# Two-layer hybrid diffusion step: a new order in layer 0's start, a weight tile split in two, value products over fewer query columns, and sums at other steps

## The chip, the cores and the metric

The kernel runs on one core of one Trainium2 chip. The metric is the device time of one execution in microseconds, lower is better; the engines are TensorE (PE), VectorE (DVE), ScalarE (ACT), GpSimd (POOL) and the queue that issues most transfers, SyncE (SP).

## What is computed

Two layers over 1152 tokens (1024 latent tokens on a 16 x 64 grid, 128 context tokens) of width 1024. Cut to what matters here:

```python
def modulate(x, cond, g, w_mod, b_mod):
    mod = jax.nn.silu(cond) @ w_mod + b_mod
    shift, scale, gate = jnp.split(mod[:, None, :], 3, axis=-1)
    return rmsnorm(x, g) * (1 + scale) + shift, gate

def latent_layer(x, c, ...):
    parts, gate = project(x, c, g, w_mod, b_mod, w_in)      # modulate(x) @ w_in, 3584 columns
    ya, yb = branches_ab(parts[:7], w_s, b_s, w_conv)        # gated MLP over positions; gated convolution
    yc = window_attn(cq, ck, cv, kc, vc, sink) * silu(cz)    # mixer C: +-128 tokens
    yd = neighbourhood_attn(dq, dk, dv, kd, vd, rpb) * silu(dz)   # mixer D
    return x + gate * (jnp.concatenate([ya, yb, yc, yd], -1) @ w_out)
```

In mixer D a query in grid row r sees eight rows of keys, from clip(r - 4, 0, 8) on, and 16 columns, beside the context keys:

```python
    def one_row(r):
        rs = jnp.clip(r - kr // 2, 0, rows - kr)             # kr = 8, rows = 16
        k_nb = jnp.take(kg, rs + jnp.arange(kr), axis=1)[:, :, col_idx]
```

After both layers comes one RMSNorm.

## The kernel before

**Products.** Everything is float32. The large projections run as three products of a rounded and a rest part: `w_hi` x `h_hi`, `w_hi` x `h_lo`, `w_lo` x `h_hi`, in the fp32r format. A weight tile is 128 output columns by 8 blocks (k) of 128 inputs; tokens go in three chunks (c) of 384. Tile w is loaded by SP into a raw buffer, ACT casts it to `w_hi[:, w % 2]` in two halves of four k (`high_half`, L281), POOL subtracts for `w_lo` (`low_half`, L287). Two tiles can be in work. A step is one tile and one chunk: 24 matmuls of 384 columns on L1088. Steps 0 to 5 are tiles 0 and 1, later three steps to a tile; the 24 steps of the output projection follow, numbered st = 0 to 23.

**The start of layer 0** (`sync_start`, `pool_start`, `scalar_start`, `tensor_start`, `vector_start`). x is squared on ACT and added on DVE, PE sums it over partitions (`sums`, L606), DVE takes 1/sqrt (`rsqrt`, L193 to L202) and writes nine diagonals (L707, signal `pro_norm[0]`), PE spreads each over all partitions with a matmul by ones (`spread`, L583, into banks 3, 4 and 5, signal `pro_norm[1]`), and ACT copies the three banks to SBUF (L547, `pro_copied`). For each k DVE then makes scaled x (L663), ACT `h_hi` (L530), DVE `h_lo` (L672) and PE the products of tiles 0 and 1 (`project`, L596), of which the one with n = 1 writes banks 3 to 5. Between them PE makes the modulation rows of block k + 3 (`make_rows`, L564), ACT copies them (`copy_row`, L524), PE turns them (`turn_row`, L575), and DVE takes them in (`take_mods`, L649 to L654). `AHEAD` is 3, so the rows of blocks 0, 1 and 2 are made ahead of the loop over k. w_mod blocks are loaded into three buffers, block k after block k - 3 has been used. POOL has only `low_half` of tiles 0 and 1 here.

**Attention.** Scores of two pairs of heads and query blocks are made at the end of steps `S_AT`, DVE adds bias and takes the maximum (L1542), ACT takes exp, DVE normalises (L1552), two steps later (`V_AT`) PE turns the probabilities ahead of k = 0 to 3 (`turn_probs`, L1108), ACT copies them, and at the end of the step PE multiplies by values (`values`, L1117), each of two heads into its half of the 128 PSUM partitions; then DVE gates (`gate_pair`, L1564). In mixer D a unit is 8 grid rows x 16 columns of queries against 12 rows x 32 columns of keys, taken in three blocks of four rows behind one block of context; masked probabilities are zero.

**Other modulation.** DVE multiplies 24 blocks of w_mod with the condition at steps `MOD_AT` (`multiply`, L1383 and L1380), the blocks loaded by SP one by one as the two buffers come free; PE sums each third over partitions at `SUM_AT` (`mod_sums`, L1143) in the middle of the step, ahead of k = 4, DVE copies it (L1395), PE turns it at `TURN_MOD_AT`, DVE adds it in (L1404). These small products share PSUM bank 7 with the value products, so each waits for the reader of the one before. Layer 1 uses only the middle third of the tables.

**Norm at the end of a layer.** From st = 1 on DVE adds squares of the new x (L1623). In step 16 PE sums the first six token blocks (`sum_tokens`, L187), DVE makes 1/sqrt and diagonals (`make_rstd`, L1365), and PE spreads them in step 17 (L1235). Every order is written out by hand; an engine does its instructions in that order and waits on semaphores.

Of the kernel before, what the change touches and what calls it, by code (L numbers as in the profile page):

```python
# [31 lines left out]
P = 128  # L32
# [5 lines left out]
KT = D_MODEL // P  # L38
# [77 lines left out]
def build(nc, xT, cond, w_mod, w_mod0, b_mod, norm_g, final_g, w_tiles, w_sT, b_s, w_conv, sink, rpb,  # L116
          cckT, ccv, cdkT, cdv, ident_c, rope_c, band_c, row_c, col_c, yT, sckT, scvT, sdkT, sdvT):
    with ExitStack() as ctx:
# [96 lines left out]
        masks_in = sem("masks_in")  # L215
        mod_taken = sem("mod_taken")
        wmod_in = [sem(f"wmod_in{i}") for i in range(3)]
        cond_tanh = sem("cond_tanh")
# [56 lines left out]

        def high_half(act, layer, w):
            s = signals[layer]
            loaded = (s.w_loaded0, s.w_loaded1, s.w_loaded2, s.w_loaded3)[raw_at(w)]
            act.wait_ge(loaded, 16 * loads_until(layer, w))
            for a, b in w_halves(w):  # L280
                nc.scalar.copy(w_hi[:, w % 2, a:b], RAW[raw_at(w)][:, a:b]).then_inc(s.hi_ready, 1)  # L281
# [7 lines left out]


        PARTS = ((LAT, 0), (CTX, 1))

# [58 lines left out]
        BLOCKS = [len(unit_values(u)) for u in range(NU)]  # L351


        BANK_S, BANK_O = 3, 7
# [7 lines left out]
        mod_row = (xy[:, 2, D_MODEL:T], xy[:, 3, D_MODEL:T])  # L362
        MOD_AT = [8, 10, 11, 13, 14, 16, 17, 18] + [23, 24, 25, 26, 28, 29, 30, 31] + [37, 38, 39, 40, 41, 42, 44, 45]
        SUM_AT = {20: (0, 0), 22: (0, 1), 33: (1, 0), 35: (1, 1), 52: (2, 0), 54: (2, 1)}
        TURN_MOD_AT = {21: (0, 0), 23: (0, 1), 34: (1, 0), 36: (1, 1), 53: (2, 0), 55: (2, 1)}

# [146 lines left out]
        def pool_start(pool):  # L513
            low_half(pool, 0, 0)
            low_half(pool, 0, 1)
            pool.wait_ge(masks_in, 16 * 3)

        def scalar_start(act):
# [6 lines left out]

            def make_high(k):
                for i, part in enumerate(first_parts(k)):
                    act.wait_ge(signals[0].scaled, first_count(k, i))
                    for cols, cnd in part:
                        last = nc.scalar.activation(h_hi[:, k, cols], first_scaled[k % 2][:, cols], ACT.Identity,  # L530
                                                    bias=mods[:, 0, k, cnd:cnd + 1])
                    last.then_inc(signals[0].h_hi_ready, 1)

# [10 lines left out]
            copy_row(1)  # L544
            for c in range(NCH):
                act.wait_ge(pro_norm[1], 3 * (c + 1))
                nc.scalar.copy(first_rstd[:, cols_of(c)], psum[:, RSTD_BANK + c, 0:CH]).then_inc(pro_copied, 1)  # L547
            copy_row(2)
            for k in range(KT):
                make_high(k)  # L550
                if k + AHEAD < KT:
                    copy_row(k + AHEAD)

        def tensor_start(pe):
# [31 lines left out]
            def project(k, c):  # L586

                if c == 0 and k % 4 == 0:
                    pe.wait_ge(s.lo_ready, k // 4 + 1)
                if k == 0 or c != 1:  # L590
                    pe.wait_ge(s.h_lo_ready, first_count(k, c if k == 0 else c // 2))
                for n in range(2):
                    if k % 4 == 0 and c == 0 and n == 1:
                        pe.wait_ge(s.lo_ready, 2 + k // 4 + 1)
                    for w, h in ((w_hi, h_hi), (w_hi, h_lo), (w_lo, h_hi)):
                        last = nc.tensor.matmul(psum[:, 3 * n + c, 0:CH], w[:, n, k, :], h[:, k, cols_of(c)],  # L596
                                                start=(k == 0 and w is w_hi and h is h_hi),
                                                stop=(k == KT - 1 and w is w_lo), skip_group_check=True)
                    if k == KT - 1:
                        last.then_inc(s.chunk_done, 1)  # L600

            def sums(c):
# [14 lines left out]
            make_rows(1)  # L617
            turn_row(1)
            for c in range(NCH):
                spread(c)  # L620
            make_rows(2)
            pe.wait_ge(pro_copied, NCH)
            for k in range(KT):
# [250 lines left out]
        def scalar_layer(act, layer):  # L874
# [162 lines left out]
            for g, (n, c) in enumerate(STEPS):  # L1037
# [5 lines left out]
                for w in range(2, N_W):  # L1043
                    if HIGH_AT[w] == g:
                        act.wait_ge(s.chunk_done, g + 1)
                        high_half(act, layer, w)
                for u in units_of(S_AT.get(g, ())):
# [34 lines left out]
        def tensor_layer(pe, layer):  # L1082
# [29 lines left out]
            def values(p):  # L1112

                u = 2 * p
                for b in range(BLOCKS[u]):
                    for r in range(2):
                        last = nc.tensor.matmul(psum[64 * r:64 * r + 64, BANK_O, values_at(p)], unit_values(u + r)[b],  # L1117
                                                prob[:, (u + r) % PROBS, b * P:(b + 1) * P], start=(b == 0),
                                                stop=(b == BLOCKS[u] - 1), skip_group_check=True)
# [182 lines left out]
            for st, (f, c) in enumerate(OUT_STEPS):  # L1302
# [5 lines left out]
                for at, k in enumerate(order):  # L1308
                    if at == 4:
                        if st == 16:  # L1310
                            sum_tokens(s, 0, 6, squares_in(15))
                    if at == 7 and st == 17:
# [519 lines left out]
```

## Time and profile before

| | |
|---|---|
| median of 3 runs | 1209.03 us (1208.07 to 1211.74) |
| profiled execution, time | 1208.2 us |
| its span, first to last instruction | 1206.4 us |
| mean granted TensorE clock | 0.994 of full speed |
| PE busy | 1162.4 us, 96% |
| DVE busy | 614.7 us, 51% |
| ACT busy | 443.1 us, 37% |
| POOL busy | 365.9 us, 30% |
| chain that ended last | 84% on PE, 67% on L1088 |

A busy share is an average; the rows below say where an engine waits and for whom. PE's matmuls are pipelined, so one matmul of 384 columns shows some 0.34 us although the next starts 0.17 us after it. A float32 matmul appears as two records.

### The profile page before, as it was taken

The numbers are of one execution on the slowest core, as the hardware profiler recorded it, in microseconds if no ns is written. First come the engines' busy times: TensorE is split into PE (matmuls) and PEld (weight loads), VectorE is DVE, ScalarE is ACT, GpSimd is POOL, SyncE is SP. The second block draws the span as 40 slices with busy tenths as digits, with TensorE's granted clock in tenths as the row PEclk, the third lists the DMA queues.
The fourth block names the chain that finished last, engine by engine and source line by source line (L and its number), as shares of the span: only waits on it lengthen the run. The fifth ranks groups of instructions, "written<-read, shape, count | busy, mean of one in ns | idle before, by whom it ended". The sixth has DMA issues, their size and how long they took to land.

```text
span 1206.4 us, 20224 instructions
## 1 busy us (share of the span) xinstructions
PE 1162.4 (96%) x8098; PEld 1100.1 (91%) x8098; DVE 614.7 (51%) x1419; ACT 443.1 (37%) x1004; POOL 365.9 (30%) x284
## 2 busy tenths in 40 slices
PE   2989999999999999999999999999999999999996
PEld 2689989989999999999999999998999999999996
DVE  5747856764764532152385354675344451334256
ACT  4433445544453111152254344544445311124231
POOL 1023231155351221223352223124434212223342
PEclk9999999999999999999999999999999999999998
DMA  8522221332320112235461111222121111222334
GB/s 347 208 64 101 96 74 56 112 109 90 115 70 18 36 52 88 80 95 163 135 201 50 63 45 38 87 87 69 62 69 37 36 36 36 87 92 80 123 109 157
DMA packets 42861, 110.80 MB, mean 92 GB/s; under 512 B 6032, under 2 KB 21520, under 8 KB 41488
## 3 DMA queue, kind: packets, MB, share of 16 engines
q1 hardware_dynamic: 38736, 105.58, 25.7%
q10 hardware_dynamic: 4032, 3.93, 0.9%
q8 instruction: 64, 1.05, 0.4%
q14 instruction: 29, 0.24, 0.1%
HBM read 99.27 MB, written 10.22 MB: 91 GB/s over the span
## 4 chain that ended last, share of the span: by engine, by line
PE 84%; DVE 3%; issue 0%; ACT 0%; DVEq 0%; ACTq 0%
PE psum L1088 67%; PE psum L1117 5%; PE psum L1100 5%; PE psum L1108 4%; PE psum L1125 1%; PE psum L1134 1%; DVE xy L1383 1%; PE psum L1235 0%; DVE slots L1472 0%; PE psum L1143 0%; DVE slots L1670 0%; DVE slots L1469 0%; DVE prob L1552 0%; DVE slots L1476 0%; PE psum L187 0%
## 5 line engine op out<-in xcount | busy, mean ns | idle before, releaser
L1088 PE MATMUL psum<-h_hi,w_hi 128*128 128x384 f32 x1680 | 586.3, 349 | 2.7 <-POOL w_lo L287 2.7
L1088 PE MATMUL psum<-h_hi,w_lo 128*128 128x384 f32 x1680 | 563.9, 336 | 0.0
L1088 PE MATMUL psum<-h_lo,w_hi 128*128 128x384 f32 x1680 | 562.8, 335 | 0.0
L287 POOL TENSOR_TENSOR w_lo<-w_raw,w_hi 128x512 fp32r<-128x512 f32 x144 | 203.2, 1432 | 647.4 <-ACT w_hi L281 647.3
L1088 PEld LDWEIGHTS psum<-h_hi,w_hi 128*128 128x128 f32 x1680 | 316.1, 188 | 21.1 <-issue 17.3
L1088 PEld LDWEIGHTS psum<-h_lo,w_hi 128*128 128x128 f32 x1680 | 316.7, 189 | 0.0
L1088 PEld LDWEIGHTS psum<-h_hi,w_lo 128*128 128x128 f32 x1680 | 315.9, 188 | 0.0
L281 ACT CAST w_hi<-w_raw 128x512 fp32r<-128x512 f32 x144 | 81.8, 618 | 166.1 <-PE psum L1088 146.6
L983 ACT ACTIVATE prob<-prob,stat 128x512 f32<-128x512 f32 (+2 forms) x144 | 96.4, 671 | 90.9 <-DVE stat L1542 90.7
L990 ACT COPY prob<-psum 128x512 f32<-128x512 f32 (+1 forms) x144 | 75.3, 544 | 27.4 <-PE psum L1108 26.9
L1383 DVE SCALAR_TENSOR_TENSOR xy<-xy,silu 128x1024 f32<-128x1024 f32 x56 | 83.1, 1524 | 3.0 <-DMA xy<-in_w_mod 1.7
L1552 DVE TENSOR_SCALAR prob<-prob,stat 128x512 f32<-128x512 f32 (+1 forms) x144 | 81.2, 564 | 6.5
L1636 DVE SCALAR_TENSOR_TENSOR xy<-psum,mods,slots 128x384 f32<-128x384 f32 (+1 forms) x64 | 31.6, 513 | 103.6 <-PE psum L1088 103.5
L1108 PE MATMUL psum<-ident,prob 128*128 128x128 f32 x512 | 79.3, 272 | 0.7 <-DVE prob L1552 0.7
L1564 DVE SCALAR_TENSOR_TENSOR xy<-psum,xy 128x128 f32<-128x128 f32 x72 | 17.8, 286 | 113.4 <-PE psum L1117 112.7
L1442 DVE SCALAR_TENSOR_TENSOR xy<-slots,psum 128x384 f32<-128x384 f32 x48 | 26.6, 554 | 94.6 <-ACT slots L973 93.5
L848 POOL TENSOR_TENSOR table<-row_mask,table 128x384 f32<-128x384 f32 x48 | 47.1, 982 | 82.8 <-DMA table<-in_rpb 82.8
L946 ACT ACTIVATE slots<-psum 128x384 f32<-128x384 f32 x60 | 29.1, 492 | 110.7 <-PE psum L1088 109.4
L1108 PEld LDWEIGHTS psum<-ident,prob 128*128 128x128 f32 x512 | 64.2, 141 | 5.8 <-issue 1.3
L973 ACT ACTIVATE slots<-psum 128x384 f32<-128x384 f32 x48 | 23.6, 492 | 120.2 <-PE psum L1088 120.2
L287 POOL TENSOR_TENSOR w_lo<-table,w_hi 128x512 fp32r<-128x512 f32 x32 | 44.0, 1395 | 64.0 <-ACT w_hi L281 64.0
L1117 PE MATMUL psum<-prob,slots 128*64 128x128 f32 x896 | 63.0, 276 | 0.0
(119 smaller groups left out, 1077.8 us busy)
## 6 DMA issues: line engine op xcount, KB each, us to landing
w_raw<-in_w_tiles SPq DMA_DIRECT2D x72, 512.0 KB, 3.3
xy<-in_w_mod SPq DMA_DIRECT2D x32, 512.0 KB, 4.3
table<-in_rpb SPq DMA_DIRECT2D x48, 192.0 KB, 3.5
slots<-in_w_mod SPq DMA_DIRECT2D x8, 1024.0 KB, 6.5
table<-in_w_tiles SPq DMA_DIRECT2D x16, 512.0 KB, 3.6
xy<-in_xT SPq DMA_DIRECT2D x8, 576.0 KB, 7.7
slots<-in_xT SPq DMA_DIRECT2D x8, 384.0 KB, 4.7
x_kept<-xy SPq DMA_DIRECT2D x8, 384.0 KB, 5.2
```

What stands on the lines that cost most here:

```text
L281: nc.scalar.copy(w_hi[:, w % 2, a:b], RAW[raw_at(w)][:, a:b]).then_inc(s.hi_ready, 1)
L287: nc.gpsimd.tensor_tensor(w_lo[:, w % 2, a:b], RAW[raw_at(w)][:, a:b], w_hi[:, w % 2, a:b], ALU.subtract).then_inc(s.lo_ready, 1)
L848: own(nc.gpsimd.tensor_tensor(tab, rows, tab, ALU.subtract))
L983: nc.scalar.activation(row, row, ACT.Exp, scale=-1.0, bias=stat[:, u % 4, 0:1], accum_out=stat[:, u % 4, 1:2]).then_inc(s.expd, 1)
L990: nc.scalar.copy(prob[:, u % PROBS, 0:n * P], psum[:, unit_bank(u), 0:n * P]).then_inc(s.copied, 1)
L1088: last = nc.tensor.matmul(psum[:, bank, 0:CH], a[:, w % 2, k, :], h[:, k, cols], start=(k == order[0] and a is w_hi and h is h_hi), stop=( ...
L1100: last = nc.tensor.matmul(psum[:, unit_bank(u + r), at:at + width], queries(u + r), src, start=True, stop=True, skip_group_check=True)
L1108: last = nc.tensor.transpose(psum[:, unit_bank(u), b * P:(b + 1) * P], prob[:, u % PROBS, b * P:(b + 1) * P], ident[:, :])
L1117: last = nc.tensor.matmul(psum[64 * r:64 * r + 64, BANK_O, values_at(p)], unit_values(u + r)[b], prob[:, (u + r) % PROBS, b * P:(b + 1) * ...
L1383: ins = nc.vector.scalar_tensor_tensor(mod_part[cnd], mod_rows[g % 2], silu[:, k, cnd:cnd + 1], mod_part[cnd], ALU.mult, ALU.add)
L1552: nc.vector.tensor_scalar(row, row, stat[:, u % 4, 2:3], None, ALU.mult).then_inc(s.normed, 1)
L1636: last = nc.vector.scalar_tensor_tensor(xy[:, f, cols], psum[:, st % 3, at], mods[:, layer, 2 * KT + f, cnd:cnd + 1], x_new[:, f % 2, cols ...
```

## The change

Six edits. (1) POOL's `low_half` of tile 1 waits for the nine diagonals. (2) In the start PE makes the rows of block 2 ahead of the spreads; ACT copies them ahead of the first spread bank, and the third spread bank is copied between the first and second high half of k = 0. PE no longer waits for all three copies ahead of k = 0; each n = 1 product of k = 0 waits for the copy of its bank. (3) ACT casts the first half of tile 2 behind the high halves of k = 6, once PE has done tiles 0 and 1 of k = 3 (`pro_half`), and only the second half at the old place. POOL's program isn't changed here, it waits for `hi_ready` as before. (4) The eight multiplies of the first third of the modulation are at steps 8, 10, 11, 13, 16, 17, 18, 19 instead of 8, 10, 11, 13, 14, 16, 17, 18, its two sums and turns one step later. (5) `values` takes only the query rows that see a key block. (6) The sums of squares of step 16 stand ahead of k number 6 of the order instead of number 4. An unused name is removed as well.

```diff
@@ -214,6 +214,7 @@
         mod_taken = sem("mod_taken")
+        pro_half = sem("pro_half")
         wmod_in = [sem(f"wmod_in{i}") for i in range(3)]
@@ -273,11 +274,11 @@
 
-        def high_half(act, layer, w):
+        def high_half(act, layer, w, halves=(0, 1)):
             s = signals[layer]
...
             act.wait_ge(loaded, 16 * loads_until(layer, w))
-            for a, b in w_halves(w):
+            for a, b in [w_halves(w)[i] for i in halves]:
                 nc.scalar.copy(w_hi[:, w % 2, a:b], RAW[raw_at(w)][:, a:b]).then_inc(s.hi_ready, 1)
@@ -350,6 +349,17 @@
 
+        def block_queries(u, b):
+
+            mixer, i, _, _ = UNITS[u]
+            if mixer == "C" or i == LT or b == 0:
+                return slice(0, P)
+            first_q = i // N_CG * QR
+            first_k = d_keys(i)[0] + (b - 1) * BLK_R
+            start = [min(max(q - WIN_R // 2, 0), ROWS - WIN_R) for q in range(first_q, first_q + QR)]
+            seen = [q for q in range(QR) if start[q] < first_k + BLK_R and start[q] + WIN_R > first_k]
+            return slice(seen[0] * QC, (seen[-1] + 1) * QC)
+
 
@@ -360,9 +370,9 @@
         mod_row = (xy[:, 2, D_MODEL:T], xy[:, 3, D_MODEL:T])
-        MOD_AT = [8, 10, 11, 13, 14, 16, 17, 18] + [23, 24, 25, 26, 28, 29, 30, 31] + [37, 38, 39, 40, 41, 42, 44, 45]
-        SUM_AT = {20: (0, 0), 22: (0, 1), 33: (1, 0), 35: (1, 1), 52: (2, 0), 54: (2, 1)}
-        TURN_MOD_AT = {21: (0, 0), 23: (0, 1), 34: (1, 0), 36: (1, 1), 53: (2, 0), 55: (2, 1)}
+        MOD_AT = [8, 10, 11, 13, 16, 17, 18, 19] + [23, 24, 25, 26, 28, 29, 30, 31] + [37, 38, 39, 40, 41, 42, 44, 45]
+        SUM_AT = {21: (0, 0), 23: (0, 1), 33: (1, 0), 35: (1, 1), 52: (2, 0), 54: (2, 1)}
+        TURN_MOD_AT = {22: (0, 0), 24: (0, 1), 34: (1, 0), 36: (1, 1), 53: (2, 0), 55: (2, 1)}
 
@@ -512,6 +522,7 @@
             low_half(pool, 0, 0)
+            pool.wait_ge(pro_norm[0], TT)
             low_half(pool, 0, 1)
@@ -523,13 +534,12 @@
 
-            def make_high(k):
-                for i, part in enumerate(first_parts(k)):
-                    act.wait_ge(signals[0].scaled, first_count(k, i))
-                    for cols, cnd in part:
-                        last = nc.scalar.activation(h_hi[:, k, cols], first_scaled[k % 2][:, cols], ACT.Identity,
-                                                    bias=mods[:, 0, k, cnd:cnd + 1])
-                    last.then_inc(signals[0].h_hi_ready, 1)
+            def make_high(k, i):
+                act.wait_ge(signals[0].scaled, first_count(k, i))
+                for cols, cnd in first_parts(k)[i]:
+                    last = nc.scalar.activation(h_hi[:, k, cols], first_scaled[k % 2][:, cols], ACT.Identity,
+                                                bias=mods[:, 0, k, cnd:cnd + 1])
+                last.then_inc(signals[0].h_hi_ready, 1)
 
@@ -542,14 +552,24 @@
             copy_row(1)
-            for c in range(NCH):
+            copy_row(2)
+
+            def copy_rstd(c):
                 act.wait_ge(pro_norm[1], 3 * (c + 1))
                 nc.scalar.copy(first_rstd[:, cols_of(c)], psum[:, RSTD_BANK + c, 0:CH]).then_inc(pro_copied, 1)
-            copy_row(2)
+
+            copy_rstd(0)
+            copy_rstd(1)
             for k in range(KT):
-                make_high(k)
+                for i in range(len(first_parts(k))):
+                    make_high(k, i)
+                    if k == 0 and i == 0:
+                        copy_rstd(2)
                 if k + AHEAD < KT:
                     copy_row(k + AHEAD)
+                if k == KT - 2:
+                    act.wait_ge(pro_half, 1)
+                    high_half(act, 0, 2, (0,))
 
@@ -590,6 +610,8 @@
                 for n in range(2):
+                    if k == 0 and n == 1:
+                        pe.wait_ge(pro_copied, c + 1)
                     if k % 4 == 0 and c == 0 and n == 1:
@@ -598,6 +620,8 @@
                         last.then_inc(s.chunk_done, 1)
+                    if (k, c, n) == (KT // 2 - 1, NCH - 1, 1):
+                        last.then_inc(pro_half, 1)
 
@@ -616,10 +640,9 @@
             turn_row(1)
+            make_rows(2)
             for c in range(NCH):
                 spread(c)
-            make_rows(2)
-            pe.wait_ge(pro_copied, NCH)
             for k in range(KT):
@@ -1043,7 +1066,7 @@
                         act.wait_ge(s.chunk_done, g + 1)
-                        high_half(act, layer, w)
+                        high_half(act, layer, w, (1,) if (layer, w) == (0, 2) else (0, 1))
                 for u in units_of(S_AT.get(g, ())):
@@ -1114,8 +1137,10 @@
                     for r in range(2):
-                        last = nc.tensor.matmul(psum[64 * r:64 * r + 64, BANK_O, values_at(p)], unit_values(u + r)[b],
-                                                prob[:, (u + r) % PROBS, b * P:(b + 1) * P], start=(b == 0),
+                        q = block_queries(u, b)
+                        at = slice(values_at(p).start + q.start, values_at(p).start + q.stop)
+                        last = nc.tensor.matmul(psum[64 * r:64 * r + 64, BANK_O, at], unit_values(u + r)[b],
+                                                prob[:, (u + r) % PROBS, b * P + q.start:b * P + q.stop], start=(b == 0),
                                                 stop=(b == BLOCKS[u] - 1), skip_group_check=True)
@@ -1306,9 +1331,8 @@
                 for at, k in enumerate(order):
-                    if at == 4:
-                        if st == 16:
-                            sum_tokens(s, 0, 6, squares_in(15))
+                    if at == 6 and st == 16:
+                        sum_tokens(s, 0, 6, squares_in(15))
                     if at == 7 and st == 17:
```

## Rows read from the trace of the kernel before

**Rows 1.** Who waited for whom, on PE: us in total, times, longest.

```profile
PE psum L596 <- DVE h_lo L672: 4.3, 4, 1.8
...
PE psum L1143 <- DVE xy L1383: 1.9, 1, 1.9
...
PE psum L187 <- DVE prob L1623: 1.4, 2, 0.7
```

**Rows 2.** Timeline of PE in the start: start us, us, instructions, idle before.

```profile
25.63 1.93 PE L564 MATMUL psum<-slots 128*32 128x256 f32 x16
28.05 0.69 PE L575 MATMUL psum<-ident,prob 128*128 128x128 f32 x2 [0.49 <-ACT prob L524]
29.85 4.21 PE L583 MATMUL psum<-slots,ones 128*128 128x128 f32 x18 [1.11 <-DVE slots L707]
33.99 1.41 PE L564 MATMUL psum<-slots 128*32 128x256 f32 x16
37.16 0.41 PE L596 MATMUL psum<-h_hi,w_hi 128*128 128x384 f32 x1 [1.76 <-DVE h_lo L672]
...
38.38 1.07 PE L564 MATMUL psum<-slots 128*32 128x256 f32 x16
...
42.97 0.44 PE L596 MATMUL psum<-h_hi,w_hi 128*128 128x384 f32 x1 [0.99 <-DVE h_lo L672]
```

**Rows 3.** Timeline of DVE in the start.

```profile
26.01 0.41 DVE L193 TENSOR_SCALAR small<-small 128x9 int32<-128x9 int32 x1
26.46 1.19 DVE L195 TENSOR_SCALAR small<-small 128x9 int32<-128x9 int32 x1
27.68 0.17 DVE L198 SCALAR_TENSOR_TENSOR small<-small 128x9 f32<-128x9 f32 x1
...
29.51 1.85 DVE L707 TENSOR_SCALAR slots<-ident,small 128x128 f32<-128x128 f32 x9
```

**Rows 4.** Timeline of ACT in the start.

```profile
31.54 0.48 ACT L547 COPY slots<-psum 128x384 f32<-128x384 f32 x1 [3.54 <-PE psum L583]
...
35.48 0.37 ACT L524 COPY prob<-psum 128x256 f32<-128x256 f32 x1 [0.90 <-PE psum L564]
```

**Rows 5.** Timeline of POOL (GpSimd) in the start.

```profile
25.13 2.49 POOL L287 TENSOR_TENSOR w_lo<-w_raw,w_hi 128x512 fp32r<-128x512 f32 x2 [1.26 <-ACT w_hi L281]
```

**Rows 6.** Instructions that read in_w_mod: time from issue to landing.

```profile
DMA to landing us min/median/max: 3.5/4.4/17.9
```

**Rows 7.** Timeline of PE at tile 2.

```profile
76.49 0.41 PE L1088 MATMUL psum<-h_hi,w_hi 128*128 128x384 f32 x1 [2.68 <-POOL w_lo L287]
...
78.65 0.42 PE L1088 MATMUL psum<-h_hi,w_hi 128*128 128x384 f32 x1
```

**Rows 8.** Timeline of ACT, k = 6 and the cast of tile 2.

```profile
64.08 1.63 ACT L530 ACTIVATE h_hi<-slots,mods 128x768 fp32r<-128x768 f32 x3 [2.65 <-DVE slots L663]
...
74.31 1.14 ACT L281 CAST w_hi<-w_raw 128x512 fp32r<-128x512 f32 x2 [0.50 <-PE psum L596]
```

**Rows 9.** Timeline of DVE, low halves of k = 6, last multiplies.

```profile
65.05 1.68 DVE L672 SCALAR_TENSOR_TENSOR h_lo<-slots,mods,h_hi 128x768 fp32r<-128x768 f32 x3 [0.35 <-ACT h_hi L530]
...
158.41 3.23 DVE L1383 SCALAR_TENSOR_TENSOR xy<-xy,silu 128x1024 f32<-128x1024 f32 x2
```

**Rows 10.** Value products on PE: timeline, then their line over the whole trace.

```profile
192.17 0.83 PE L1117 MATMUL psum<-prob,slots 128*64 128x128 f32 x12
...
L1117 PE MATMUL psum<-prob,slots x896: 270/273/324, 119.4 to 952.4; 128*64 128x128 f32 x180
```

**Rows 11.** Sums of step 16: PE timeline, a window (PEclk), chain in both layers.

```profile
589.59 1.50 PE L187 MATMUL psum<-ones,prob 128*128 128x1 f32 x12 [0.71 <-DVE prob L1623]
...
592.00:594.00 2.00, 2.00 (x8) 2.00 (x7) 1.72 (x10) 0.00 (x0) 0.00 (x0) 0.50 0.80 251
...
591.09 7.40 PE psum L1088 x33
...
1159.35 5.83 PE psum L1088 x33
```

More of the change, by code:

```diff
@@ L288, in low_half @@
                                         ALU.subtract).then_inc(s.lo_ready, 1)
-        PARTS = ((LAT, 0), (CTX, 1))
         def pieces(c):
```

## The prediction

> **What bounds the kernel now.** I read the table of busy shares first: TensorE (PE) is busy in 96% of the span, so the end moves only by time that PE waits or by work that it no longer does. Then the list of waits [rows 1]: inside the kernel PE waited 4.3 us in four places for a low half of h (L672), 1.9 us for VectorE's (DVE's) multiplies of the modulation weights (L1383), and 1.4 us in two places for squares (L1623); at 76.49 it waited 2.68 us for GpSimd's low half of a weight tile (L287) [rows 7]. Then the timeline of the first 45 us [rows 2 to 5], because before PE runs full it is fed by a chain: sums of squares, a 1/sqrt on DVE, nine diagonals, nine spread products (L583), three copies on ScalarE (ACT), scaled x, high half, low half, product. PE waits 1.76 us for that chain at 37.16 and 0.99 at 42.97 [rows 2]; the other 1.5 of the 4.3 us come in the last two steps of the same loop, k = 6 and 7. Last, the pieces around the value products and the sums of squares [rows 8 to 11]. Elsewhere PE has no wait of half a microsecond before the tail after the last product, which the change doesn't touch.
>
> **Start, GpSimd's second tile moved behind the diagonals.** DVE's L193 and L195 took 0.41 and 1.19 us, where the same kind of tiny step right behind them takes 0.17 [rows 3]; the two L287 of tile 1 ran on GpSimd from 25.13 for 2.49 us [rows 5]. With L287 behind the ninth diagonal the two steps cost 0.17 each: 0.24 + 1.02 = 1.26 us earlier, so diagonals run from 28.25 to 30.1. L287 then ends near 32.7; it is first needed by the n = 1 product at 35. It hides behind PE's spreads, and can hold up DVE's first scale by 0.2 us, which ACT's queue hides.
>
> **Start, order of PE and ACT.** Now PE does spreads, then the third row product (33.99 to 35.40), ACT copies that row (35.48) and only then makes the first high half [rows 2, 4]. After the change: turn at 28.05, row product from about 28.5 to 30.3 (1.8 us, as at 25.63), spreads from 30.3 to 34.5 (4.2 us as now), three per 1.4 us. Does the third row block have its weights by then? The longest landing of any w_mod transfer is 17.9 us [rows 6], and the third was issued at about 9 us: 26.9 at the latest, so yes. ACT copies the row at 30.5, the first spread copy ends at 32.4, the second at 33.7; then comes the first high half, 33.7 to 34.3, DVE's low half ends at 35.0, and PE's first product starts at 35.15 instead of 37.16. The third copy (34.5 to 35.0) goes between the high halves, DVE scales the third part behind it and its last low half ends at 37.4 instead of 39.3. Both shifts are 1.9 to 2.0 us; from k = 1 on the loop repeats as before, 4.7 us a step. **Gain 1.9.** The new waits of the n = 1 products on a copy end before the h_lo wait that stands ahead of them. Bounds: 0.4 (the reorder gives nothing and GpSimd's move is partly eaten) to 2.3.
>
> **Third tile halved.** Now tile 2 starts at 76.49 after 2.68 us of idleness, and its fifth k at 78.65 [rows 7]. ACT's cast of both halves starts at 74.31, behind five copies and a store [rows 7, 8]. With k = 0 to 3 prepared ahead, PE starts those 12 products at once (73.7 on the old clock of events, 2.1 us of work), then waits for the second half: one cast from 74.31, one L287 of 1.25, ready at 76.45. So k = 4 starts at 76.5 instead of 78.65: **gain 2.2**; a wait of some 0.7 us on L287 is left at k = 4. The first half's buffer is free after k = 3, its load has long landed, and ACT waits 2.65 us before a high half of the late k anyway [rows 8], so the cast of 0.6 is hidden there.
>
> Its subtraction on GpSimd isn't. The cast follows the high half of k = 6, which ends at 65.71 [rows 8], so it becomes ready at 66.4, while DVE is in the low halves of k = 6 (L672, two SBUF inputs, to 66.7) [rows 9], and DVE is what PE waits for there. The nearest row is L195 above: a tiny op that had to wait about a microsecond for a running L287. I charge 1.1 us (L287 from 66.7 to 67.95 less the 0.15 us that DVE's next op would need to read PSUM first), bounds 0 and 1.3. **Loss 1.1.**
>
> The Trainium skill, "SBUF — State Buffer", section "SBUF: two separate sides", says that VectorE with two SBUF inputs and GpSimd hold a shared port pair for a whole instruction and the other blocks fully. The L195 row agrees (1.02 us lost, less than one L287), and by that rule the charge would be at most one L287, 1.25.
>
> **Modulation multiplies and sums.** The multiply of step 14 goes to the end (now 16 to 19), sums from steps 20 and 22 to 21 and 23, turns to 22 and 24. Now the eighth multiply ends at 161.64 (158.41 + 3.23) [rows 9], PE asks for it in the middle of step 20 and waits 1.9 [rows 1]. Without the multiply at 14 DVE runs some 2.5 us ahead from step 16 on, does one more pair at 19, and ends near 163, while the sum is now asked for one step later, behind the values and scores of step 20, near 167. The wait goes whole: **gain 1.9**. What is queued: DVE's copy of a sum stands behind the bias and scale work of step 20, finished near 168.1, and PE needs it in step 22, 171; the first multiply of the next third waits for the sum in step 23 and has 25 to follow. SP's loads of these rows follow the multiplies and land in 4.4 us (median) [rows 6], in time. Bounds 0.5 to 2.2.
>
> **Fewer queries in value products.** In mixer D a key block of four rows is seen by a part of the eight query rows: for the upper half of the grid the third block has 48 columns instead of 128, for the lower half 64, 128 and 112. Per layer 8 pairs of either kind, so 16 and 16. Every product is two records, and the two heads of a pair run side by side on halves of the array: 12 records in 0.83 us, one takes 0.27, so five intervals in 0.56, 0.11 us a record and half [rows 10]. 128 columns twice at 2.4 GHz are 0.107, so columns set it. Weights set a floor: records of one column with 128 weight columns follow each other at (1.50 - 0.27)/11 = 0.112 [rows 11]; 64 weight columns are estimated at half, 0.058. So 48 and 64 columns save 0.051 a record, 112 save 0.013. Sum: 16 x 2 x 0.051 + 16 x 2 x (0.051 + 0.013) = **3.7 us**. Bounds: 4.3 if columns alone count (80 columns x 4 passes / 2.4 x 32 pairs), and 0.4 if the floor stays at 0.112, as it would if the halves' weights load one after the other. I take 3.7 because the two halves' records overlap in the row. PE has no wait in the D stretches, so nothing takes the time back: turns start a whole product step after the scores, and that distance isn't shortened.
>
> By the Trainium skill, "TensorE: Matmul & The Clock Gate", section "LDWEIGHTS", a load takes columns / 1.2 ns, so 53 ns for 64; the sum would be about 3.9. The same page, "Part 3", says that loads overlap running matmuls only in another row group; these have one row group, every record would then pay load and columns, and the saving would be the full 4.3. The row at 0.11 a record shows no such addition.
>
> **Sums of squares at k = 6.** In each layer's step 16 PE waits 0.7 [rows 1], now it does six more products (1.05 us) first and the squares are there: 2 x 0.71 = **1.4 us**. The 1/sqrt chain gets 0.35 us later, and the spreads at step 17 come 0.7 earlier; the diagonals are done several us before in layer 0, and in layer 1 they end just as PE arrives. Bounds 0.9 to 1.4. Beside this, in layer 0 the 33 products behind the sums took 7.40 us, in layer 1 the same 33 took 5.83 [rows 11]; from 592 to 594 the granted clock was 0.50, which is 1.2 GHz, after PE's 0.71 us of waiting and 1.5 us of one-column products. With the waiting gone I take it that the clock stays: **gain 1.6**, bounds 0 and 1.6, and below nothing if the drop comes in both layers (-1.6).
>
> **Sum.** 1.9 + 2.2 - 1.1 + 1.9 + 3.7 + 1.4 + 1.6 = 11.6. The profiled run took 1208.2 (span 1206.4), so 1196.6; the median of the runs is 0.8 above it: 1197.4.
>
> **Rivals.**
> 1. The clock still drops behind one of the sums: 1197.4 + 1.6 = 1199.0. For: the one-column products remain. Against: layer 1 had the same row without a drop. 0.25.
> 2. Weight loads bound the clipped products: 3.7 becomes 0.4, 1200.7. 0.12.
> 3. GpSimd's early subtraction costs DVE nothing: 1196.3. 0.06.
> 4. The start doesn't do what it says: since the row product now stands ahead of the spreads, the first product moves little, 1.5 us less, 1198.9. 0.05.
> 5. Slower than before: until 35 us PE runs at half rate (the row product took 1.93 at 25.63 and 1.07 at 38.38 [rows 2], though the granted clock of the stretch reads 1.00). It rose while spreads and a row product ran without a pause. If the new order, with its pauses between 34.5 and 41, kept the half rate, every k would cost 9.4 instead of 4.7 us. Less 1.4 of idle time at k = 0, it outweighs the 11.6 from the third k on, and at four k it gives 1197.4 + 17 = 1214. Against: after 2.68 us of idleness at 76.49 products ran at full rate. 0.02.
> Forecast 0.48; anything else 0.02, about no change.
>
> **Numbers.** Range: from 1194.5 (rival 3, the upper bounds of start and values) to 1202.0 (rivals 1 and 2 together). A measurement of this kernel tells 0.3%, 3.6 us, from no change. All cases but rival 5 and a pile of losses are faster by more: 0.94, same 0.04, slower 0.02.
>
> **What would show it.** First product (L596) at 35.2; L193 and L195 at 0.17; a wait of L1088 on L287 of about 0.7 instead of 2.7; an L287 near 64.5 with DVE held beside it; no L1143 on L1383; no wait of L187, and 33 products in 5.8 us in both layers; two pairs of L1117 (32 records) nearer 1.7 than 1.9 us in D. It is wrong if the clipped records keep 0.11, or if a half rate stands in new places.

## The result, and the profile after it

The changed kernel takes 1196.62 us (median of 4 runs, 1195.61 to 1197.13), the kernel before beside it 1209.43 (1208.07 to 1211.74): a ratio of 0.990, 95% interval 0.988 to 0.992. That is faster by 12.8 us; the forecast was 1197.4 in a range of 1194.5 to 1202.0.

PE's busy time went from 1162.4 to 1158.0 us, so of the 11 us by which the span shrank (1206.4 to 1195.3) some 7 are waits that are gone, and 4 are work. From the page of the changed kernel:

```profile
span 1195.3 us, 20227 instructions
...
PE 1158.0 (97%) x8098; PEld 1096.9 (92%) x8098; DVE 619.7 (52%) x1419; ACT 443.0 (37%) x1004; POOL 365.9 (31%) x284
```

Its waits on PE (total us, times, longest), to be read against [rows 1]; lines have moved by some 25, so L618 is the old L596, L1111 the old L1088, L1168 the old L1143:

```profile
...
PE psum L618 <- DVE h_lo L695: 4.7, 4, 1.9
PE psum L1260 <- DVE prob L1389: 2.8, 1, 2.8
PE psum L1251 <- ACT slots L1093: 1.6, 1, 1.6
PE psum L595 <- ACT prob L535: 0.5, 1, 0.5
PE psum L1111 <- POOL w_lo L288: 0.5, 1, 0.5
PE psum L1131 <- DVE prob L1576: 0.4, 1, 0.4
...
```

The waits ahead of the old L1143 and of L187 are gone from the list, L1111 on GpSimd fell from 2.68 [rows 7] to 0.5. The wait on low halves didn't fall: 4.7 for 4.3, and its longest is at a new place.

Three timelines follow: PE in the start, DVE in the start and at k = 6, and GpSimd from the start to tile 2.

```profile
30.21 3.11 PE L603 MATMUL psum<-slots,ones 128*128 128x128 f32 x18
34.50 0.41 PE L618 MATMUL psum<-h_hi,w_hi 128*128 128x384 f32 x1 [1.17 <-DVE h_lo L695]
```

```profile
25.69 0.17 DVE L193 TENSOR_SCALAR small<-small 128x9 int32<-128x9 int32 x1
25.90 0.17 DVE L195 TENSOR_SCALAR small<-small 128x9 int32<-128x9 int32 x1
...
27.95 1.85 DVE L730 TENSOR_SCALAR slots<-ident,small 128x128 f32<-128x128 f32 x9
...
62.42 2.74 DVE L695 SCALAR_TENSOR_TENSOR h_lo<-slots,mods,h_hi 128x768 fp32r<-128x768 f32 x3 [0.35 <-ACT h_hi L540]
```

```profile
29.88 2.49 POOL L288 TENSOR_TENSOR w_lo<-w_raw,w_hi 128x512 fp32r<-128x512 f32 x2 [6.34 <-DVE slots L730]
63.72 1.29 POOL L288 TENSOR_TENSOR w_lo<-w_raw,w_hi 128x512 fp32r<-128x512 f32 x1 [31.35 <-ACT w_hi L282]
75.00 1.28 POOL L288 TENSOR_TENSOR w_lo<-w_raw,w_hi 128x512 fp32r<-128x512 f32 x1 [9.99 <-ACT w_hi L282]
```

L193 and L195 are at 0.17, as forecast (0.41 and 1.19 in [rows 3]). The spreads took 3.11 us, not 4.2: their records went from 0.21 to 0.11 us apart in their middle. The low halves of k = 6 took 2.74 us for 1.68 [rows 9], beside GpSimd's early 63.72. PE from k = 7 on, and then a window from 70.0 to 72.5 (busy time and count of PE, PEld, DVE, ACT and POOL, then the granted clock, 0.50, DMA share and GB/s):

```profile
68.83 0.45 PE L618 MATMUL psum<-h_hi,w_hi 128*128 128x384 f32 x1 [1.94 <-DVE h_lo L695]
...
70.02 0.53 PE L618 MATMUL psum<-h_hi,w_lo 128*128 128x384 f32 x1
...
76.34 0.44 PE L1111 MATMUL psum<-h_hi,w_hi 128*128 128x384 f32 x1 [0.47 <-POOL w_lo L288]
```

```profile
70.00:72.50 2.50, 2.50 (x9) 2.50 (x9) 0.00 (x0) 1.13 (x3) 0.00 (x0) 0.50 0.00 0
```

At 0.50, which is 1.2 GHz, products start 0.32 us apart instead of 0.17. Ten or eleven of them cost 1.5 to 1.6 us here. In the kernel before such a stretch stood behind the sums of layer 0 [rows 11].

I read all traces by the same marks: the distance from one PE instruction to a later one, so that what happened before doesn't count. The marks are PE's first matmul (19.51 before, 19.19 after), the first product, first product of k = 7, the fifth k of tile 2 (t2k4), the first products of later steps, and the last one. The end of a step is the first product of the next.

| stretch on PE | before | changed | gain |
|---|---|---|---|
| first matmul to first product | 17.65 | 15.31 | 2.34 |
| first product to k = 7 | 33.25 | 34.33 | -1.08 |
| k = 7 to t2k4 | 8.24 | 7.51 | 0.73 |
| t2k4 to the end of step 24 | 116.71 | 114.30 | 2.41 |

The rest of the offset: 1.9 us over the value products of each layer, 2.14 from step 16 of layer 0 to the end of the layer, 0.58 from there in layer 1. The question was which of these belong to the change, since one half rate is worth as much as an edit.

### The profile page after: what moved, and what is told of

The parts are those of the page before. It is cut to its first block, busy times and chain, and to the rows that moved or that the text cites. A ratio compares the mean times of both kernels' runs of the same rounds, so it can differ in the third digit from the quotient of the medians.

```text
span 1195.3 us, 20227 instructions
## 1 busy us (share of the span) xinstructions
PE 1158.0 (97%) x8098; PEld 1096.9 (92%) x8098; DVE 619.7 (52%) x1419; ACT 443.0 (37%) x1004; POOL 365.9 (31%) x284
## 4 chain that ended last, share of the span: by engine, by line
PE 88%; DVE 3%; issue 0%; DVEq 0%; ACT 0%; ACTq 0%
PE psum L1111 70%; PE psum L1123 5%; PE psum L1142 5%; PE psum L1131 5%; PE psum L1150 1%; PE psum L1159 1%; PE psum L1260 0%; DVE slots L1496 0%; PE psum L1168 0%; DVE slots L1694 0%; DVE slots L1493 0%; DVE small L202 0%; DVE small L200 0%; DVE slots L1500 0%; DVE xy L1407 0%
## 5 line engine op out<-in xcount | busy, mean ns | idle before, releaser
L1111 PE MATMUL psum<-h_hi,w_hi 128*128 128x384 f32 x1680 | 585.8, 349 | 0.5 <-POOL w_lo L288 0.5
L1111 PE MATMUL psum<-h_hi,w_lo 128*128 128x384 f32 x1680 | 563.5, 335 | 0.0
L1111 PE MATMUL psum<-h_lo,w_hi 128*128 128x384 f32 x1680 | 562.1, 335 | 0.0
L1111 PEld LDWEIGHTS psum<-h_hi,w_hi 128*128 128x128 f32 x1680 | 315.7, 188 | 18.8 <-issue 14.3
L1111 PEld LDWEIGHTS psum<-h_lo,w_hi 128*128 128x128 f32 x1680 | 316.3, 188 | 0.0
L1111 PEld LDWEIGHTS psum<-h_hi,w_lo 128*128 128x128 f32 x1680 | 315.4, 188 | 0.0
L1142 PE MATMUL psum<-prob,slots 128*64 128x128 f32 (+3 forms) x896 | 59.1, 268 | 0.0
```

Of the source, the lines that this page charges most:

```text
L1111: last = nc.tensor.matmul(psum[:, bank, 0:CH], a[:, w % 2, k, :], h[:, k, cols], start=(k == order[0] and a is w_hi and h is h_hi), stop=( ...
L1142: last = nc.tensor.matmul(psum[64 * r:64 * r + 64, BANK_O, at], unit_values(u + r)[b], prob[:, (u + r) % PROBS, b * P + q.start:b * P + q. ...
```

## Experiments

But for the late subtraction and the second round of the changed kernel (four runs each), each kernel ran once. The kernel before ran beside each group: seven times beside the first four runs below (median 1207.79 us, 1205.39 to 1211.43), once, with 1205.31, beside the value products, the 16 columns, GpSimd's wait and the sums alone, and once, with 1211.13, beside the other four. Single times that lie within a few us of these say little, and those readings rest on the marks in each trace. "On before" means the edit alone in the kernel before, "on changed" means taken back or altered in the changed kernel.

### Where GpSimd's early subtraction stands

On changed: it waits for the last low half of the start.

```diff
             pool.wait_ge(masks_in, 16 * 3)
+            pool.wait_ge(signals[0].h_lo_ready, first_count(KT - 1, len(first_parts(KT - 1)) - 1))
```

> The changed kernel, with GpSimd's early subtraction for tile 2 waiting for the last low half of h of the start. Theory A (the subtraction held VectorE's last low half of k = 6 for one GpSimd instruction, PE then idled 1.94 us ahead of k = 7, and that idle time dropped the clock to half rate for 11 products): the wait ahead of k = 7 returns to about 0.9 us, no half rate follows, the first product of k = 7 comes 1.1 us earlier, k = 4 of tile 2 comes 2.5 us earlier, time near 1194.1. Rival B (the half rate comes from something else in the start): only 1.1 us at k = 7, half rate still there, time near 1195.5. Rival C (DVE or ACT behind it takes the time back): 1196.6 as the changed kernel.

```profile
68.76 0.44 PE L619 MATMUL psum<-h_hi,w_hi 128*128 128x384 f32 x1 [0.87 <-DVE h_lo L696]
74.72 0.44 PE L1112 MATMUL psum<-h_hi,w_hi 128*128 128x384 f32 x1 [0.47 <-POOL w_lo L288]
```

1195.3 us (median of 4; 1195.19 to 1195.77), ratio to before 0.989 (0.988 to 0.991). First product to k = 7 is 33.29 again, so the 1.08 us are the collision of GpSimd's subtraction with the low halves on DVE, and this kernel is faster than the changed one, at no cost elsewhere. The changed kernel itself ran beside it:

> The changed kernel itself, for comparison on the same chip: 1196.6, 12 to 13 us below the kernel before. If the half rate at 69.7 to 72.9 is tied to the 1.94 us of idleness it is there again.

```profile
69.31 0.44 PE L618 MATMUL psum<-h_hi,w_hi 128*128 128x384 f32 x1 [1.94 <-DVE h_lo L695]
75.27 0.44 PE L1111 MATMUL psum<-h_hi,w_hi 128*128 128x384 f32 x1 [0.46 <-POOL w_lo L288]
```

```profile
70.00:72.50 2.50, 2.50 (x16) 2.50 (x15) 0.00 (x0) 2.23 (x5) 0.00 (x0) 1.00 0.00 0
```

1196.57 us (median of 4; ratio 0.9905, 0.9885 to 0.9925). Same program, same wait of 1.94 us, and the granted clock stayed at 1.00: 16 records in the window for 9. So theory A of the late subtraction falls in the part that the wait brings the half rate each time. k = 7 to t2k4 is 5.96 here and 5.96 with the late subtraction. The late subtraction is worth the 1.1 us ahead of k = 7 and nothing behind it.

Filling PE's wait, on changed: eight products into an unread bank ahead of k = 7.

```diff
             for k in range(KT):
+                if k == KT - 1:
+                    for _ in range(8):
+                        nc.tensor.matmul(psum[:, ROW_BANK, 0:CH], w_hi[:, 1, 4, :], h_hi[:, 0, cols_of(0)],
+                                         start=True, stop=True, skip_group_check=True)
                 project(k, 0)
```

> The changed kernel with eight extra products of 384 columns (into a PSUM bank that nobody reads) ahead of k = 7, so that PE works through most of its 1.94 us wait; DVE is held up as before. They add work without a result. Theory A (idle time drops the clock): k = 7 starts as late as in the changed kernel, but at full rate, and tile 2's k = 4 comes 1.6 us earlier; time 1195.0. Rival B (half rate has another cause): products of k = 7 stay at 0.32 us each, time 1196.6 or more.

1195.54 us. k = 7 began 34.32 us after the first product, as in the changed kernel, and ran at full rate. Inconclusive: so did the changed kernel without the filling, in its second trace.

### The split of tile 2

On changed: tile 2's cast whole, at its old place.

```diff
-                if k == KT - 2:
-                    act.wait_ge(pro_half, 1)
-                    high_half(act, 0, 2, (0,))
...
-                        high_half(act, layer, w, (1,) if (layer, w) == (0, 2) else (0, 1))
+                        high_half(act, layer, w)
```

> The changed kernel without the split of tile 2's cast (both halves at the old place). From the offsets between the two traces the split gained nothing net: no held VectorE (1.1), no half rate (1.6), but the 2.7 us wait of PE at tile 2 back. Theory A: k = 4 of tile 2 within 0.3 us of the changed kernel's 76.3, time 1196.6 to 1196.9. Rival (the split gains 1.1, as predicted): 1.1 us later, 1197.7.

```profile
68.19 0.44 PE L615 MATMUL psum<-h_hi,w_hi 128*128 128x384 f32 x1 [0.90 <-DVE h_lo L690]
74.29 0.41 PE L1106 MATMUL psum<-h_hi,w_hi 128*128 128x384 f32 x1 [2.68 <-POOL w_lo L288]
```

1197.48 us. First product to t2k4 took 41.55 us; in the second trace of the changed kernel 40.37. The split gains 1.2: 2.3 from k = 7 on (8.28 to 5.96), 1.1 back through the collision. My expectation, drawn from one pair of traces, was wrong, and the term of the prediction (2.2 - 1.1) was right: the first trace of the changed kernel had a half rate just there.

### The start

GpSimd's wait alone, on before:

```diff
             low_half(pool, 0, 0)
+            pool.wait_ge(pro_norm[0], TT)
             low_half(pool, 0, 1)
```

> The kernel before with GpSimd's second tile behind the nine diagonals, alone. Diagonals start 1.26 us earlier after the sums. Theory: the first product comes 1.26 us earlier against the sums (spreads, copies and row follow). Rival: the row product and the copy of the row take part of it back.

```profile
28.43 4.21 PE L584 MATMUL psum<-slots,ones 128*128 128x128 f32 x18
```

1209.44 us. The first spread came 9.10 us after the first matmul, for 10.34 to 10.36 in all five traces with the old start: 1.25 us earlier, the term of 1.26. From there to the first product the time depends on when the clock first rises: 16.49 us after the first matmul here, and 17.65, 17.33, 17.96, 16.74 and 16.94 in the five (mean 17.3). Against the first three, whose spreads took 4.21 us as here, it is 0.8 to 1.5 us earlier. On DVE L664, the first scale, took 1.07 us for 0.62, beside GpSimd's 30.03, but in this order that costs PE nothing: it ended at 31.7, and ACT's high half started only at 34.41, behind the copy of the row.

GpSimd's wait taken out of the changed kernel:

```diff
             low_half(pool, 0, 0)
-            pool.wait_ge(pro_norm[0], TT)
             low_half(pool, 0, 1)
```

> The changed kernel without GpSimd's wait for the diagonals. Theory: in the new order the spreads start at about 30.2, behind the row product, and the diagonals would be ready at about 29.7 even with L193 and L195 slowed, so the first product moves by 0 to 0.2 us. Rival (additive, as my sum took it): 1.3 us later.

```profile
26.47 1.19 DVE L195 TENSOR_SCALAR small<-small 128x9 int32<-128x9 int32 x1
...
29.53 1.85 DVE L729 TENSOR_SCALAR slots<-ident,small 128x128 f32<-128x128 f32 x9
31.43 1.29 DVE L685 SCALAR_TENSOR_TENSOR slots<-xy,mods,slots 128x384 f32<-128x384 f32 x2
```

1194.89 us, the lowest single time of a kernel that leaves nothing out: 13.99 us to the first product, where seven traces with the whole new start have 15.05 to 15.80 (mean 15.35). Not later but earlier. L195 is slow again, and it costs nothing, because the row product now stands ahead of the spreads. Part of the 1.4 us is the clock, which rose earlier here. The rest is seen beside two traces in which the spreads ran at full rate too (2.27 us in all three), that of the filling and that of the 16 columns below. Their first two scales:

```profile
31.16 2.11 DVE L690 SCALAR_TENSOR_TENSOR slots<-xy,mods,slots 128x384 f32<-128x384 f32 x2 [1.41 <-ACT slots L559]
```

```profile
32.16 1.72 DVE L686 SCALAR_TENSOR_TENSOR slots<-xy,mods,slots 128x384 f32<-128x384 f32 x2 [1.80 <-ACT slots L559]
```

With GpSimd's work moved to 29.83 to 32.33 and 30.44 to 32.94, the first two scales take 2.11 and 1.72 us instead of 1.29. The filling is the closer partner, since its clock had risen as early (row product ahead of the spreads 1.44 us, for 1.35): its first spread came 10.53 us after the first matmul, for 10.44, but its first product 15.05, for 13.99. So GpSimd's wait moves the collision instead of removing it: from the reciprocal root, where there is slack now, to the first scale, where there is none once the clock is up. Where the clock rose later, as in the first trace of the changed kernel, the scales began behind GpSimd's 32.37 and took 0.62 us each. The new start gains 2.0 us (17.3 to 15.35), and in the new order GpSimd's wait adds nothing to them; that it takes up to 1 us away rests on one trace without it.

### Multiplies and sums of the modulation

On before, the three tables alone:

```diff
-        MOD_AT = [8, 10, 11, 13, 14, 16, 17, 18] + ...
-        SUM_AT = {20: (0, 0), 22: (0, 1), ...}
-        TURN_MOD_AT = {21: (0, 0), 23: (0, 1), ...}
+        MOD_AT = [8, 10, 11, 13, 16, 17, 18, 19] + ...
+        SUM_AT = {21: (0, 0), 23: (0, 1), ...}
+        TURN_MOD_AT = {22: (0, 0), 24: (0, 1), ...}
```

> The kernel before with the multiplies, sums and turns at their new steps, alone. Theory: the 1.9 us wait of L1143 goes, and the 0.3 us wait of L1108 at step 18 with it; offset between steps 18 and 24 2.0, with 0.3 to 0.45 ahead of them, 2.4 together. Rival (the wait moves to another place, step 21 or 23): under 1.

```profile
162.31 0.94 PE L1100 MATMUL psum<-slots 64*128 64x128 f32 x12
163.08 0.39 PE L1100 MATMUL psum<-ck_c,slots 64*128 64x128 f32 x4
...
165.69 0.64 PE L1143 MATMUL psum<-xy,ones 128*32 128x256 f32 x8
```

1203.48 us. The sum now stands a step later, with no wait ahead of it. t2k4 to the end of step 24 is 114.27, for 116.71 and 116.42 in two traces of before: 2.1 to 2.4. The term was 1.9; the rest is the wait of 0.3 of L1108 (the turn of the probabilities) at step 18, which stood in the trace and which I had left out.

### Value products

On before, with `block_queries` alone:

```diff
-                        last = nc.tensor.matmul(psum[64 * r:64 * r + 64, BANK_O, values_at(p)], unit_values(u + r)[b],
-                                                prob[:, (u + r) % PROBS, b * P:(b + 1) * P], start=(b == 0),
+                        q = block_queries(u, b)
+                        at = slice(values_at(p).start + q.start, values_at(p).start + q.stop)
+                        last = nc.tensor.matmul(psum[64 * r:64 * r + 64, BANK_O, at], unit_values(u + r)[b],
+                                                prob[:, (u + r) % PROBS, b * P + q.start:b * P + q.stop], start=(b == 0),
```

> The kernel before with the shorter value products alone. Prediction's term: 3.7 us. In the traces of the whole change the offset grew by 1.9 us over each layer's D stretch. Theory: offset at the end 3.7, none before 250 us; time 1204.7. Rival (weights are the floor at 0.112): 0.4, 1208.

1205.44 us, with 1205.31 for the kernel before beside it, so the time shows nothing here, and the marks do. From the end of step 24 to the end of the D stretch of layer 0 it took 191.14 us for 192.99, and over layer 1 up to step 16 of its output projection 527.93 for 529.76: 1.85 + 1.83 = 3.7 us, the term to the tenth.

On changed, every key block cut to 16 query columns, which leaves out most of these products and asks only what a short record costs:

```diff
-            return slice(seen[0] * QC, (seen[-1] + 1) * QC)
+            return slice(seen[0] * QC, (seen[0] + 1) * QC)
```

> The changed kernel with every key block of mixer D multiplied for 16 query columns only, which leaves out most of those products. It asks what bounds a short record: if the 64 weight columns are the floor at 0.057 a record and half, the D stretches shorten by a further 32 x 6 x 0.052 less what the change took (3.7), 6.3 us; if moving columns alone counted (0.013 + 0.003 a record), 14 us.

1189.31 us. The D stretches shortened by a further 3.41 in layer 0 and 3.40 in layer 1, 6.8: near the 6.3 of the weight floor, half of the 14 of columns alone. So shorter blocks than 64 columns would hardly pay here. The same two pairs in D before and in the changed kernel, 1.98 and 1.72 us:

```profile
277.87 1.98 PE L1117 MATMUL psum<-prob,slots 128*64 128x128 f32 x32
```

```profile
272.75 1.72 PE L1142 MATMUL psum<-prob,slots 128*64 128x128 f32 x32
```

Single records of one half follow each other at 0.11 us with 128 columns, 0.095 with 112, 0.058 with 64, and with 48 at 0.042 ahead of an equal record and 0.058 ahead of one of 128 columns. With 16 columns they stay at 0.058, where columns alone (16 twice at 2.4 GHz) would make it 0.013: that is the floor.

### Sums of squares, and the half rate

On before, edit 6 alone:

```diff
-                    if at == 4:
-                        if st == 16:
-                            sum_tokens(s, 0, 6, squares_in(15))
+                    if at == 6 and st == 16:
+                        sum_tokens(s, 0, 6, squares_in(15))
```

> The kernel before with the sums of squares ahead of k number 6 instead of 4, alone. Theory: the wait of 0.7 goes in both layers (1.4 us), and without idle time ahead of the one-column products the clock stays at its high level in both (1.6 more in layer 0): 33 products in 5.8 us twice; offset 3.0. Rival: the one-column products drop the clock by themselves now and then, with no regard to the wait: a half rate behind them in one of the layers, offset 1.4 or less.

1205.96 us. Its chain of waits in step 16 and 17 of layer 0:

```profile
590.10 1.25 PE psum L187 x12
...
593.27 1.31 DVE small L198
594.58 0.02 issue
594.60 1.23 DVE small L200
...
596.40 1.60 PE psum L1235 x12
```

No wait ahead of the sums, no half rate behind: from the product ahead of them to the product behind them 1.43 us, for 2.41 with the wait. But two of DVE's tiny steps took 1.31 and 1.23 us instead of 0.17: the reciprocal root is now later against GpSimd's next subtraction and meets it:

```profile
593.25 2.56 POOL L287 TENSOR_TENSOR w_lo<-table,w_hi 128x512 fp32r<-128x512 f32 x2 [2.39 <-ACT w_hi L281]
```

PE waits 0.24 us ahead of the spreads, and they take 1.60 instead of 1.34; from the product ahead of them to the one behind, 1.94 instead of 1.43. That is 0.98 won and 0.51 lost a layer. From step 16 to the end of layer 0 two traces with the old sums and no half rate give 36.95 (tables alone, value products alone), this one 36.51: 0.44. The same comes out in six of the seven traces of the changed kernel and its variants that have the new sums (36.51 to 36.53). Only in the first one was it 0.58 (36.37), since DVE was held for less.

The kernel before once more, unchanged:

> The kernel before itself, once more. Asks whether its half rate behind the sums of layer 0 (590.9 to 594.5) belongs to the program or comes and goes. Theory from the runs so far: half rate follows a wait of PE of 0.7 us or more, or the one-column sums behind such a wait, in some executions only (sums with the wait: 3 of 6 places; sums without: none of 14). Then it may stand behind the sums of layer 0 or 1, at tile 2, or nowhere. Rival (fixed by the program): again at 591 and only there.

And the changed one with the sums at k number 4:

> The changed kernel with the sums of squares ahead of k number 4 again. Theory: the 0.7 us wait is back in both layers, 0.6 us net a layer, and each of the two places may be followed by a half rate of 1.6 us: offset after the changed kernel 1.2, 2.8 or 4.3. Rival (edit 6 has nothing to do with the clock): 1.2, and half rates as rare as behind the sums without the wait.

```diff
-                    if at == 6 and st == 16:
-                        sum_tokens(s, 0, 6, squares_in(15))
+                    if at == 4:
+                        if st == 16:
+                            sum_tokens(s, 0, 6, squares_in(15))
```

Chain of the kernel before in its second trace (7.39: half rate; 5.83: none), then of the changed kernel with the sums at number 4 (both layers at half rate):

```profile
590.63 7.39 PE psum L1088 x33
...
1158.91 5.83 PE psum L1088 x33
```

```profile
584.85 7.40 PE psum L1111 x33
...
1151.24 7.42 PE psum L1111 x33
```

1207.79 and 1201.73 us. Behind sums that PE had to wait for, the half rate came in 6 of 12 places: layer 0 in both traces of before and with GpSimd's wait alone, layer 1 with the value products alone, both layers in this last, neither with the tables alone. Behind sums without the wait it came in 0 of 16 places, in eight traces. It also came behind the 2.68 us wait at tile 2 in 2 of 7 traces (17 and 9 products), and behind the 1.94 us wait at k = 7 in 2 of 5, never behind the 0.9 us wait at k = 7 (8 traces). In one trace more, that of the value products alone, it came from 39.0 to 42.4, within k = 0, behind the pause of 1.76 us ahead of the first product, and k = 7 began 0.3 us later for it. So the half rate goes with a pause of PE, but is no fixed part of a program. The last run is 5.1 us above the changed kernel, 4.3 at the marks as expected: two half rates and twice 0.5.

## Why the prediction was right, point by point

- **Start, 1.9.** Measured 2.0 as the difference of two means, and 2.34 in the profiled pair, where the clock rose earlier after the change. Where the spreads ran near one rate (4.21 us in three traces with the old start; 3.97 and 4.09 with the new one, late subtraction and second trace) it is 1.5 to 2.2 (17.33, 17.65 and 17.96, to 15.80), around the term. The wrong part is which edit earns it. The working began with 1.26 for GpSimd's wait. In the old order that holds (1.25 at the first spread). In the new order the wait has no use, as the run without it shows, since the spreads stand behind a row product that ends later than the slow diagonals (L729 began at 29.53). I had all the times for this: 29.7 for the first diagonal, 30.3 for the spreads. The total stood, because the first product was worked out through the row product, which doesn't ask for the diagonals. The 0.2 us by which GpSimd's work was to hold DVE's first scale, hidden by ACT's queue, is too small where the clock is up: 0.8 us for two scales (2.11 for 1.29), and the first product came later by it. L195, which the prediction named as agreeing with the rule on two SBUF inputs, has one; rows with two are L198 and L200 (1.31 and 1.23 us for 0.17), and the scales.
- **Tile 2, 2.2 and -1.1.** Measured 2.3 and -1.1. The wait that is left on L287 was put at 0.7 and is 0.5.
- **Modulation, 1.9.** Measured 2.1 to 2.4.
- **Values, 3.7.** Measured 3.7. The rival that the loads of the two halves stand in line is out, and the floor that columns alone don't see is there: 0.058 us a record with 16 moving columns. By the Trainium skill, "TensorE: Matmul & The Clock Gate", section "LDWEIGHTS (loading the stationary operand)", a load takes columns / 1.2 ns, which makes an estimate of 53 ns for 64 columns of weights; the measured 58 is near it. Its rule in "Part 3" that a load overlaps only with another row group doesn't hold for these records: they share one, and at 128 moving columns they are 0.11 us apart, less than 0.107 for the columns and 0.053 for the load one after the other.
- **Sums, 1.4.** Mis-sized: 0.9 for both layers in seven of eight traces, 1.2 in the profiled one. The step that failed was "the diagonals are done several us before in layer 0": that distance was one of a layer at half rate, and moving a chain later on DVE moved it onto GpSimd's subtraction, which I had priced in the start and forgot here.
- **Half rate, 1.6.** The cause, PE's wait, was right; that it acts each time was not. It comes in about half of the executions at each of the two places, so the edit takes away some 1.6 us on average over the two layers, where I had all of it in layer 0. That the size came out is luck: two places at half the chance for one at the full. In the profiled trace of the changed kernel it came at k = 7 instead, so the profiled pair has one half rate on either side and gains nothing by this term; without those 1.5 us the span of 1195.3 would be 1193.8. Rival 1, the drop behind the new sums, didn't occur.
- **Sum.** 2.0 + 1.2 + 2.3 + 3.7 + 0.9 + 1.6 = 11.7 by the experiments, 11.6 forecast, 12.8 between the medians. The terms that were off (modulation 0.4 up, sums 0.5 down) cancel. The missing 1.1 us is within what half rates and the clock's first rise move between executions of one kernel (1205.31 to 1211.74 for the one before). A smaller slip: the cases named for the ends of the range give 1195.3 and 1202.3, not 1194.5 and 1202.0.

Not tried: the late subtraction together with the start without GpSimd's wait. By their marks it would be near 1194, an estimate from 1194.89 less the 1.1 us of the collision.

## What to carry to other kernels

Tiny DVE steps that met a GpSimd subtraction took 1.16 to 1.31 us here instead of 0.17, and two scales 2.11 instead of 1.29, so moving either one moves the collision: look at what it meets at the new place, in every chain that becomes later, and put it where the chain has slack. When two edits shorten the same chain, work out the new times with both and then with each one left out: here one of the two had no share in the gain. And don't read the worth of an edit from one pair of traces, as long as stretches at half rate come and go: compare distances between marks in stretches that have none, and count the half rates over all traces.

## What was not expected of the hardware

- The same program, with the same wait of 1.94 us, had a granted clock of 0.50 from 70.0 to 72.5 us in one execution and 1.00 in another; each such stretch covers 9 to 11 products and costs some 1.5 us. Once it was 17 products (75.6 to 81.1, with GpSimd's wait alone).
- Mean granted clock and time go together over the executions of one kernel: the one before took 1205.31 and 1205.39 us at 0.996, and 1211.43 and 1211.13 at 0.991 and 0.990.
- The clock's first rise also moves: spreads of one order took 2.27 to 4.09 us in different executions, with the first product up to 0.8 us apart. The records' granted clock reads 1.00 throughout that time, though a row product took 1.93 us in it for 1.07 later [rows 2].
